# Routing spread over more turns, sample products on four column groups, six expert rows instead of eight, and two weight chunks kept for the second pass

## What is computed

```python
# layer 0 mixer                                 # layer 1 mixer
z = gelu(x @ w_in); u, v = split(z)             b, c, h = split(x @ w_in)
v = layer_norm(v)                               z = c * h
y = (u * (w_s @ v + bias)) @ w_out              y = (b * conv3(z)) @ w_out
# both layers, per token and each of 8 heads
q = x @ w_query
s = q . sub_keys            # 2 sides x 128 keys
best 16 of each side, best 16 of their 256 sums -> 16 experts, softmax weights g
out += sum_k g_k * gelu(expert_u[k] . x) * expert_v[k]
```

## The kernel before

| stage | turns |
|---|---|
| pass 1: v, u, mix, out, q | 5 to 20, 21 to 28, 29 to 31, 32 to 47, 51 to 59 |
| routing of layer 0, tiles 1 and 2 | 55 to 86 |
| pass 2: bch, out, q | 67 to 78, 80 to 83, 86 to 97 |
| routing of layer 1, tile 0 | 90 to 107 |
| pass 3: bch, out, q | 147 to 158, 160 to 167, 171 to 182 |
| routing of layer 1, tiles 1 and 2 | 175 to 197 |

## Time and profile before

### The profile page before, as it was taken

The page is one execution under the profiler, slowest core; times in us unless marked ns, Lnnn a source line. Parts: engine busy times, 40 slices in busy tenths (PEclk is TensorE's granted clock), DMA queues, the critical chain, the costliest instruction groups (busy, mean ns, idle before and its releaser), DMA issues.

```text
span 1878.1 us, 17585 instructions
## 1 busy us (share of the span) xinstructions
PE 1578.5 (84%) x5856; PEld 888.3 (47%) x5856; DVE 1166.6 (62%) x2913; ACT 406.3 (22%) x1202; POOL 646.0 (34%) x580
## 2 busy tenths in 40 slices
PE   7987999899895999977777799999867777777776
PEld 6884557655582765643222177457423222222211
DVE  1328946555688867689545545667996555555554
ACT  1113222111322312223112211132322211111111
POOL 0012233243332333333444442343334444444442
PEclk9998999899997999998999999999989999999989
DMA  8779999999999999999999999999989999999997
GB/s 322 271 266 407 372 377 420 390 358 423 421 396 371 412 421 422 421 409 342 423 421 395 421 395 421 386 414 416 352 344 415 413 422 422 422 422 421 422 400 290
DMA packets 103820, 734.96 MB, mean 391 GB/s; under 512 B 12369, under 2 KB 12881, under 8 KB 15506
## 3 DMA queue, kind: packets, MB, share of 16 engines
q0 software_dynamic: 82944, 604.02, 79.0%
q1 hardware_dynamic: 20018, 127.92, 17.1%
q10 hardware_dynamic: 768, 1.91, 0.3%
HBM read 732.28 MB, written 1.52 MB: 391 GB/s over the span
## 4 chain that ended last, share of the span: by engine, by line
PE 44%; DMA 36%; DVE 15%; issue 2%; ACT 1%; DVEq 1%; POOL 0%; ACTq 0%; POOLq 0%
DMA uvring<-expert_uv_dram,idx 33%; PE psum L564 23%; PE psum L574 9%; DVE uvring L1024 7%; PE psum L644 6%; PE psum L598 4%; DMA wring<-w_chunks_dram 1%; ACT diag L778 1%; DMA arena<-ln_bias_dram 1%; DVE ti L854 1%; DVE scores L848 1%; DVE wgt L1032 1%; DVE ti L843 1%; DVE picked L891 0%; DVE pick L888 0%
## 5 line engine op out<-in xcount | busy, mean ns | idle before, releaser
L564 PE MATMUL psum<-uvring,diag 128*128 128x512 f32 (+1 forms) x2160 | 1038.8, 626 | 267.0 <-ACT diag L778 236.6
L535 POOL DMA_INDIRECT uvring<-expert_uv_dram,idx x576 | 645.8, 1121 | 1208.2 <-PE psum L564 1009.4
L1024 DVE SCALAR_TENSOR_TENSOR uvring<-uvring,xn 128x1024 f32<-128x1024 f32 x576 | 704.7, 1224 | 504.8 <-DMA uvring<-expert_uv_dram,idx 498.6
L564 PEld LDWEIGHTS psum<-uvring,diag 128*128 128x128 f32 (+1 forms) x2160 | 388.1, 188 | 837.0 <-issue 438.1
L778 ACT ACTIVATE diag<-ident,wgt 128x128 f32<-128x128 f32 x476 | 166.8, 394 | 676.4 <-DVE wgt L1032 673.0
L574 PEld LDWEIGHTS psum<-xT,wring 128*128 128x128 f32 x2304 | 296.8, 193 | 30.1 <-issue 26.9
L574 PE MATMUL psum<-xT,wring 128*128 128x160 f32 (+1 forms) x2304 | 300.7, 289 | 1.7 <-DMA wring<-w_chunks_dram 1.0
L766 ACT ACTIVATE a_gelu<-a_raw 128x2 f32<-128x2 f32 x288 | 58.5, 203 | 376.2 <-DVE uvring L1024 375.7
L644 PE MATMUL psum<-wring,arena 128*128 128x256 f32 (+1 forms) x576 | 129.7, 380 | 0.8 <-issue 0.6
L644 PEld LDWEIGHTS psum<-wring,arena 128*128 128x128 f32 (+1 forms) x576 | 93.0, 163 | 45.1 <-issue 17.8
L695 ACT ACTIVATE arena<-psum 128x128 f32<-128x128 f32 (+3 forms) x168 | 47.8, 299 | 243.8 <-PE psum L574 140.5
(11 more groups left out here) (83 smaller groups left out, 575.9 us busy)
## 6 DMA issues: line engine op xcount, KB each, us to landing
wring<-w_chunks_dram SPq DMA_DIRECT2D x112, 1024.0 KB, 9.1
uvring<-expert_uv_dram,idx POOLq DMA_INDIRECT x576, 11.1
gain<-gains_dram SPq DMA_DIRECT2D x4, 512.0 KB, 13.7
x<-x_tok_dram SPq DMA_DIRECT2D x2, 512.0 KB, 8.9
uvring<-ln_gain_dram SPq DMA_DIRECT2D x2, 512.0 KB, 7.5
uvring<-ln_bias_dram SPq DMA_DIRECT2D x2, 512.0 KB, 8.6
keys<-sub_keys_dram SPq DMA_DIRECT2D x2, 512.0 KB, 7.6
keys<-sub_keys_dram SPq DMA_DIRECT2D x1, 1024.0 KB, 10.3
```

The source lines that it names most:

```text
L535: pool.indirect_dma_start(uvring[:, n % RING, :], None, expert_uv, bass.IndirectOffsetOnAxis(ap=idx[t][:, i:i + 1], axis=0),).then_inc(uv_ ...
L564: mm = nc.tensor.matmul(acc[0:r, c * 512:(c + 1) * 512], diag[:, place % DIAGS, 0:r], uvring[:, n % RING, D + c * 512:D + (c + 1) * 512], ...
L1024: nc.vector.scalar_tensor_tensor(out=uvring[:, slot, 0:D], in0=uvring[:, slot, 0:D], scalar=1.0, in1=xn[t][:, :], op0=ALU.mult, op1=ALU.mu ...
```

## The change

- **Pacing.** VectorE takes at most one routing part in a turn, unless the call's deadline is nearer than its remaining parts plus three turns; then routing goes first.
- **Quartered sample products.** Tile 2 leaves the ordinary v and out products. Its eight products over the depth are written to four groups of 32 partitions (`quarter_sums`: two of the eight to each group). ScalarE copies the bank to `quarters`, and one matmul with `fold` adds the four groups (`vf`, `of`). Two v chunks share one bank, one copy, one fold and one gelu.
- **Ring.** `RING` goes from 8 to 6, which frees 16 KB of each partition.
- **Kept chunks.** The first two chunks of each layer get buffers of their own (`kept`, 16 KB of each partition) and are loaded once, not once for each pass. At the start five chunks are loaded without a wait, before x of tiles 1 and 2.

```diff
+KEEP = 2
+RINGED = [n for n in range(PASS_CHUNK0[-1]) if n - max(p for p in PASS_CHUNK0 if p <= n) >= KEEP]
-RING = 8
+RING = 6
...
         for c in range(8):
-            for t in tiles:
-                out.append(("PE", ("v", c, t), row, [x_read]))
-                out.append(("ACT", ("v read", c, t), 0.4, [("v", c, t)]))
+            out.append(("PE", ("v", c, tiles[0]), row, [x_read]))
+            out.append(("ACT", ("v read", c, tiles[0]), 0.4, [("v", c, tiles[0])]))
+            if n == 0:
+                continue
+            if c % 2 == 0 and c:
+                out.append(("PE", ("vf", c // 2 - 1), 0.9, [("vq read", c // 2 - 1)]))
+                out.append(("ACT", ("vf read", c // 2 - 1), 0.6, [("vf", c // 2 - 1)]))
+            out.append(("PE", ("vq", c), row / 2, [x_read]))
+            if c % 2:
+                out.append(("ACT", ("vq read", c // 2), 0.6, [("vq", c)]))
...
-                if len(mine) == 2 and e == "DVE":
-                    k = mine[1][0][1]
-                    late = due(k) - p - (9 - k[4] if k[0] == "route" else 0) // 2 < 4
-                    mine = mine[::-1] if late else mine
+                if e == "DVE" and mine and mine[-1][0][1][0] == "route":
+                    k = mine[-1][0][1]
+                    if due(k) - p < 9 - k[4] + 3:
+                        mine = mine[::-1]
+                    elif parts:
+                        mine = mine[:-1]
...
+                if c < KEEP:
+                    if n == PASS_CHUNK0[2 * l] + c:
+                        if l:
+                            unused(PASS_CHUNK0[1] + c)
+                        sp.dma_start(kept[:, c, :, :], w_chunks[LAYER_CHUNK0[l] + c]).then_inc(kept_landed[c], 16)
+                    return
+                r = RINGED.index(n)
+                if r >= WRING:
+                    unused(RINGED[r - WRING])
...
+            def quarter_sums(key, at, act, w, start, stop):
+                b0 = G[key][1] * 512 + at
+                for kk in (0, 2, 4, 6, 1, 3, 5, 7):
+                    f = 32 * (kk // 2)
+                    mm = nc.tensor.matmul(psum[f:f + 32, b0:b0 + WCOLS], act[:, kk, :], w[:, kk, :],
+                                          start=start and kk % 2 == 0, stop=stop and kk % 2 == 1)
+                return mm
...
+                elif kind in ("vf", "of"):
+                    from_ = ("vq" if kind == "vf" else "oq", *k[1:])
+                    scalar_has_read(from_)
+                    open_group(k)
+                    cols = 2 * WCOLS if kind == "vf" else WCOLS
+                    nc.tensor.matmul(bank(k, cols, 32), fold[:, :], quarters[:, 0:cols], start=True, stop=True
+                                     ).then_inc(group_done, 1)
```

More of the change, by code:

```diff
@@ L153, in mixer_steps @@
         for h in range(2 if l == 0 else 1):
[L154 to L157, removed]
+            out.append(("PE", ("out", l, c, h, tiles[0]), row, [gated]))
+            if 2 in tiles:
+                out.append(("PE", ("oq", l, c, h), row / 2, [gated]))
+        out.append(("DVE", ("add", l, c, tiles[0]), 0.85, [("out", l, c, 1 - l, tiles[0])]))
+        if 2 in tiles:
+            out.append(("ACT", ("oq read", l, c), 0.5, [("oq", l, c, 1 - l)]))
+            out.append(("PE", ("of", l, c), 0.5, [("oq read", l, c)]))
+            out.append(("DVE", ("add", l, c, 2), 0.85, [("of", l, c)]))
     norm("ffn", lambda t: ("add", l, 3, t))
@@ L268, in plan_steps @@
                 _, k, cost, _ = mine[0].pop(0)
-                spent += cost
+                spent, parts = spent + cost, parts + (k[0] == "route")
                 turn[k] = p
@@ L302, in plan_groups @@
     for k in planned("DVE", ("gate", "add")):
-        vector[("mix" if k[0] == "gate" else "out", *k[1:])] = len(vector) + 1
-    for k in planned("PE", ("xT", "v", "u", "bch", "q", "s", "mix", "out")):
+        vector[("of", *k[1:3]) if k[0] == "add" and k[3] == 2 else
+               ("mix" if k[0] == "gate" else "out", *k[1:])] = len(vector) + 1
+    for k in planned("PE", PE_STEPS):
         key = group_of(k)
@@ L312, in plan_groups @@
     done = 0
-    for k in planned("PE", ("xT", "v", "u", "bch", "q", "s", "mix", "out")):
-        if k[0] == "out" and k[3] < 1 - k[1]:
+    for k in planned("PE", PE_STEPS):
+        if k[0] in ("out", "oq") and k[3] < 1 - k[1] or k[0] == "vq" and k[1] % 2 == 0:
             continue
@@ L321 @@
 G = plan_groups()
+QUARTERS = [(k[0][:2], *k[1:]) for k in planned("ACT", ("vq read", "oq read"))]
 def plan_chunks():
@@ L329, in plan_chunks @@
         if l == 0:
-            after += [("group", ("v", c, tiles[-1])) for c in range(8)]
+            for c in range(8):
+                parts += n == 1 and c % 2 == 0
+                after.append(("group", ("v", c, 0)) if n == 0 else ("group", ("vq", c // 2)) if c % 2
+                             else ("part", parts))
             after += [("group", ("u", n, per * c + per - 1)) for c in range(8)]
@@ L337, in plan_chunks @@
                 after.append(("part", parts))
-            after.append(("group", ("out", l, c, tiles[-1])))
+            after.append(("group", ("oq", l, c) if 2 in tiles else ("out", l, c, tiles[-1])))
         after += [("group", ("q", n, per * c + per - 1)) for c in range(8)]
@@ L436, in trunk @@
         w_landed = [sem(f"w_landed{r}") for r in range(WRING)]
+        kept_landed = [sem(f"kept_landed{c}") for c in range(KEEP)]
         part_used = sem("part_used")
```

71 lines of the change are left out of this document (54 added, 17 removed).

## The result

The changed kernel takes 2087.5 us (2083.9 to 2098.5), against 1877.0 for the kernel before beside it: a ratio of 1.114, 95% interval 1.109 to 1.119. It is 210 us slower. I had predicted 1886 with a range to 1913, so the prediction was wrong by far more than its range.

The account below looks back on a forecast made before the run. Bound by bytes at 422 GB/s except where TensorE or VectorE binds. Terms: 1879.9 - 9.9 - 1.4 + 2 - 32 + 36 + 12 + 2 = 1888.6, less 2.2 to the median: 1886 us, range 1856 to 1913.

Parts of the forecast that it names:

- How fast can it land?: Row loads, issue to landing: 5.6 to 6.0 us, against 5.84 available with six slots; 0.1 us in hand assumed.
- The loop: Even row loads, six slots: two turns (9.96 us) hold the landing plus 4.12 us from landing to next issue.
- Rival B: Six slots don't carry full rate: each of 171 lone turns loses 0.1 us, 17 us; 1918 us, chance 0.17.
- Routing turns with six slots: Lone turns with routing: parts overrun the little time in hand, +36 us (29 to 47) over 9.2 calls.
- Mixed turns: Turns with a weight chunk: even loads have 11 us, two loads need 8 to 10; +2 us (0 to 10).
- Pacing: Routing turns on VectorE: one part a turn instead of two removes their present loss, -32 us.
- Quartering: Sample products on TensorE: eight take 1.7 us instead of 3.64, v stage packed tighter; +2 us (-2 to +10).
- Kept chunks: Weight loads: four of 1.05 MB go, -9.9 us, or 5 if two lie where TensorE binds.
- Boundaries: Four tile boundaries after lone turns: late loads that eight slots mostly absorbed now cost more, +12 us (8 to 13).
- A: Faster: row loads land in 4.5 us with fewer in flight, 1.3 us in hand; 1852 us, chance 0.25.
- C: Sample products: the four groups don't overlap for 256 columns, eight stay at 3.6 us; 1910 us, chance 0.06.
- D: Routing parts still come in pairs, or bytes are saved where TensorE binds; about 1893 us, chance 0.10.

Follow-up runs that it names:

- Weights first: Changed kernel, still six slots, with VectorE weighting a pair's products before the next even dot instead of behind it: 1986.5 us, ratio 1.057.
- quarters alone: Kernel before, ring of eight, with only the quartered sample products added, old routing rule, no kept chunks: 1883.1 us, ratio 1.004.
- eight slots: Changed kernel with a ring of eight instead of six and no kept chunks: 1851.2 us, ratio 0.986 to the kernel before.

## Why the prediction was wrong

**The step that failed** is "How fast can it land?". I took 5.6 to 6.0 us from the earlier trace rows, loads issued after an idle stretch, and wrote that "the ring of six just carries the full rate, with 5.84 - 5.6 = 0.24 us in hand". In the changed kernel's stretch without routing the even loads took 7.5 us on average, and 8.0 where the leg was my 4.12. So it is not 0.1 us in hand but 2 us short in two turns, 1 us a turn, and that is the 6.06 that the trace shows. The rows that I used are near the lower end of what the changed kernel has too (6.1 of 6.1/8.3/9.9). The trace of before could not price the landing at full rate, since there a load lies behind three others and its 10.8 us are queueing. The bound should have run from 5.6 to 10.8, and the range with it. I had put it between 5.6 and 6.0, from three loads.

**The loop was right**, and so was the leg of 4.12 us where TensorE ran at full clock; with the dips it was 4.60 on average, and the landings shorter. Rival B had this mechanism, with its deciding point (5.84) and its 171 lone turns; its price was 0.1 us a turn where 1.07 was measured: 182 us, not 17. I had given it the size of the rows' scatter.

**Routing turns with six slots**, +36: the part of the 182 us in turns 50 to 66, 97 to 147 and 183 to 223 is 111. They lose 1.05 us a turn and those without routing 1.1, so most of it is the short loop and not an overrun. Weights first shows that routing has a part of its own: with the loop just long enough, the routing window stays at 359 GB/s.

**Mixed turns**, +2 (0 to 10): 50 us. I held 11 us to be enough for two loads beside a chunk. In turns 147 to 160 the changed kernel's row loads take 9.2 us in the median and 14.0 at most, so some took longer than the 11. Weights first takes back only 8 of the 50, so this loss has a second part that I didn't find.

**Pacing**, -32: right in size for a ring of eight, where the rule is worth 31.9 us. With six slots it was not measured alone: with the rest of the change it made the ring of six 15 us faster (2102.2 to 2087.5). The even stretch stays at the byte bound, and routing turns come up to 418 GB/s.

**Quartering**, +2 (-2 to +10): 7 us, inside its range. The product was mis-sized. Groups of sample products and folds after (the earlier trace rows has them before), and one product in TensorE's timeline:

```profile
L627 PE MATMUL psum<-wring,arena 128*32 128x256 f32 x192 | 12.8, 385 | 0.0
L627 PE MATMUL psum<-wring,xT 128*32 128x256 f32 x96 | 7.0, 386 | 0.0
L678 PE MATMUL psum<-quarters,fold 128*32 128x256 f32 x16 | 5.0, 391 | 1.2 <-ACT quarters L774 1.2
L678 PE MATMUL psum<-quarters,fold 128*32 128x512 f32 x8 | 4.2, 605 | 0.0
L627 PE MATMUL psum<-kept,xT 128*32 128x256 f32 x32 | 2.1, 385 | 0.0
```

```profile
227.57 1.07 PE L627 MATMUL psum<-wring,xT 128*32 128x256 f32 x16
228.57 3.72 PE L651 MATMUL psum<-wring,xT 128*128 128x256 f32 x16
```

72.8 us became 21.9 and 9.2 of folds: 1.07 us a product, not 1.7, and not the 0.91 of full overlap. TensorE has 42 us less to do, and still the kernel with quarters alone is slower. The window of its v stage (159 to 281 us) is at 392 GB/s with TensorE busy throughout, where the first of the earlier trace rows had 385, and turns 4 to 21 last 8 us longer: more work was packed beside them, as the prediction had it, but that this is the whole of the 7 us is not shown.

```profile
159.00:281.00 122.00, 122.00 (x598) 76.52 (x597) 97.81 (x290) 41.67 (x105) 39.18 (x34) 1.00 0.98 392
```

By the Trainium skill's page TensorEngine Tiling (Array Packing), section Theoretical Speedup, up to 4x was to be had; the trace agrees nearly, with 3.64 to 1.07 us, 3.4x. The 0.91 worked out from it was the better price, but the -2 us that I had hung on it did not come.

**Kept chunks**, -9.9 (5 to 9.9): the bytes went; the one measurement of their worth, 6.5 us for 3.67 MB on eight slots, allows either end. **Start**, -1.4: not seen. The first row load is issued at 137 us, where it was 135. **Boundaries**, +12: they can't be told apart in a stretch that is short everywhere; this stays open.

**Rivals.** A (landing in 4.5 us) is excluded: no load of the listed stretch landed in under 6.1, and the fastest row load of the whole changed kernel took 5.3. By the Trainium skill's page DMA: Bandwidth & Descriptors (Anatomy of one DMA) the estimate was 4.4; the 5.3 is the nearest to it in the traces from which landings can be read. C is excluded by the 1.07 us. D is excluded by the bytes and by the 32 us of pacing. Without the ring my terms give 1879.9 + 2 - 32 - 2.2 = 1848, and 1851 was measured: the terms of the ring carry the whole error, the landing most of it and the mixed turns 50 us.

## What to carry to other kernels

Before a ring of buffers is shortened, work out what the loop leaves for the transfer, and then price the transfer at full rate. A load issued after an idle stretch gave a price near the lowest in these traces; in a trace in which queueing hides the true one, carry both ends into the range, for a loop that is short by 1 us is short in every turn. If buffers must go, look first for work that stands between a landing and the slot's release and can wait: moving one small operation ahead of a dot was worth 101 us with six slots, 40 with seven and 12 with eight.

## What the runs showed of the hardware

With fewer loads in flight the data engines didn't deliver the same bytes sooner. Packets of 8 KB, from the traces' records of the windows above without routing (1490 to 1750, 1750 to 2050, 1705 to 1865 and 1560 to 1740 us):

```
                        mean us   over 0.35 us   busy share of 16 engines
before                   0.314         0.1%        1.01
after                    0.343        11.1%        0.91
six slots, weights first 0.315         0.7%        1.01
eight slots              0.314         0.0%        1.01
```

Half of the missing rate is idle engines (0.91 for 1.01) and half is packets that take twice as long (those over 0.35 us have a mean of 0.61). In the 4.1 us between the dots of 1850.23 and 1854.36 above, 13 to 17 packets were under way at any time, and those that began from 1851.5 to 1853.0 took 0.3 to 0.7 us on average. The first of the 16 engines finishes a load some time before the last, 1.6 us in the median of the changed kernel's listed loads (0.5 to 3.6) and 2.1 in the kernel before (1.3 to 2.6). So a load is late while the engines look nearly busy, and a busy share of 0.91 goes with 0.82 of the rate. What in the engines makes a packet slow when few loads are queued was not tested; that it goes with the time in hand, and is gone at 8.0 us, is what the runs show.
